# The two gate products of a recurrence, from two full-array fp32 matmuls to four quarter-array matmuls, with one result on swapped partition halves

## The chip, the cores and the metric

The kernel runs on one core of one Trainium2 chip. The metric is the device time of one execution, in microseconds. TensorE (PE) does the matmuls, PEld is its weight load, VectorE is DVE, ScalarE is ACT, GpSimd is POOL, and SyncE (SP) issues most of the DMAs. PSUM has eight banks here, written `ps[:, bank, :]`, each 128 partitions by 512 fp32 values.

## The reference

A trunk block over 512 tokens of width 1024: a mixer with three branches (banded attention, a spatial gate, a gated linear recurrence), then a mixture of 16 experts. The change touches only the two gates of the recurrence, whose matrices are block diagonal: 8 blocks of 64 by 64 over 512 channels.

```python
def block_diag_linear(x, w, bias):
    b, s, _ = x.shape
    y = jnp.einsum('bshi,hij->bshj', x.reshape(b, s, C_BLOCKS, C_BLOCK_DIM), w)
    return y.reshape(b, s, C_WIDTH) + bias

def rg_lru(x, w_a, b_a, w_x, b_x, lam):
    r = jax.nn.sigmoid(block_diag_linear(x, w_a, b_a)).astype(jnp.float32)
    i = jax.nn.sigmoid(block_diag_linear(x, w_x, b_x))
    log_a = -LRU_C * r * jax.nn.softplus(-lam.astype(jnp.float32))
    a = jnp.exp(log_a)
    mult = jnp.sqrt(jnp.maximum(-jnp.expm1(2.0 * log_a), 0.0))
    bterm = mult * (i * x).astype(jnp.float32)
    _, h = lax.associative_scan(_lin_rec_combine, (a, bterm), axis=1)
    return h.astype(x.dtype)
```

## The kernel before

Everything lies transposed in the stage that matters: channels on the partitions, the 512 tokens along the free dimension. The 512 channels of the recurrence are four groups of 128, and each group holds two of the 64-channel blocks. The stage runs over four pairs `j` (`NPAIR` = 4). One pair is two attention heads, 128 channels of the spatial gate and 128 channels of the recurrence. Each pair has five weight blocks, r = XR, KK, QQ, UU, XG. For a block TensorE does 24 matmuls of 512 columns (L1052 to L1054: the fp32 product is made of three, with a high and a low part of each operand). ACT makes the high part of a weight block three blocks ahead (`split_hi`, L371), and POOL the low part (`split_lo`, L383). After the four pairs comes the stage of the branch gates (`B_GATE`), whose first quarter holds the last steps of attention.

Between the blocks of pair `j` each engine does, in its own fixed order, a step of the attention of pair `j-1`: scores on TensorE (L1146, a head's 64 partitions of `kT` and `qT` for each product, the two heads in two PSUM banks), bias and maximum on DVE (L1582 to L1599), exponential on ACT (L738), normalising on DVE (L1608, L1610), transposes on TensorE (L1157) and the product with v (L1174, 128 partitions by 64 weight columns, the two heads in the two partition halves of one bank).

The gates come in the same order. Behind block QQ, TensorE multiplies `conv` (128 channels by 512 tokens, plain fp32) by `wa_diag` and by `wx_diag`, two 128 by 128 matrices in whose diagonal quarters the blocks lie and which are zero elsewhere (L1199 into bank 2, L1201 into bank 3). In step UU, ACT takes them: L810 makes `rgate`, L813 `igate`, then L818 `decay` and L822 `rgate` again. DVE goes on in `recurrence_in`: L1643 needs `igate`, L1646, L1647 and L1649 need L822, and behind them in DVE's order stand L1608 and L1610 of the attention. In step XG, ACT does a square root (L827) and a gelu (L829), each with a table load; in the next XR, DVE's L1661 makes the product of the branch, and the attention goes on. Every engine runs its list in program order; semaphores hold an instruction until what it needs is done.

In the profile one fp32 matmul of the program is two MATMUL records. The three-part matmuls are one record each. The buffer named `igate_decay` holds `igate` and `decay`.

## Time and profile before

| | us |
|---|---|
| median of 3 runs | 791.48 |
| lowest, highest | 791.05, 791.95 |
| the profiled execution | 791.86 |
| its span in the trace | 789.3 |
| TensorE busy | 764.9 (97% of the span) |
| DVE, ACT, POOL busy | 493.4, 450.4, 208.8 |

The page of the profile gives busy time and the chain of work that ended last. The timeline lists instructions with start, length and what ended an idle time before them; the list of waits sums these idle times. A TensorE record starts when its matmul enters the array, and its length includes the way through it, so a stream is measured from start to start and not by the lengths.

### The profile page before, as it was taken

Reading aid. Unit: us, or ns where it says so; the run is one execution under the profiler, and the core shown is the slowest. Engines: PE = TensorE matmul, PEld = TensorE weight load, DVE = VectorE, ACT = ScalarE, POOL = GpSimd, SP = SyncE. Lnnn points to the kernel's source line nnn. Section 1 sums busy time; section 2 is a strip of 40 time slices with the busy share of each in tenths; the row PEclk is TensorE's granted clock in tenths of the full one; section 3 lists DMA queues with packets and bytes.
Section 4 is the critical chain, followed back from the end, with each engine's and each line's share of the span. In section 5 each row is a group of like instructions: output and inputs, shape, how many; then the busy total and the mean of one; then the engine's idle time right before and its main releaser. Section 6 shows DMA issues by size and latency. Waiting matters only on the chain.

```text
span 789.3 us, 10839 instructions
## 1 busy us (share of the span) xinstructions
PE 764.9 (97%) x3739; PEld 622.0 (79%) x3739; DVE 493.4 (63%) x702; ACT 450.4 (57%) x590; POOL 208.8 (26%) x124
## 2 busy tenths in 40 slices
PE   7999999999999999999999999999999999999994
PEld 4788777777787888888888788887778888888782
DVE  5704476576644302322022668999999999999888
ACT  5244656565553323323221546887888887888862
POOL 3644433232233444344442522000000000000033
PEclk9999999999999999999999999999999999999998
DMA  8569999782122253323327537999999999999965
GB/s 299 183 215 386 365 333 388 276 329 81 54 81 81 81 193 100 108 81 105 102 86 264 194 114 275 404 409 408 409 410 409 409 410 409 409 409 356 395 253 205
DMA packets 134318, 206.74 MB, mean 262 GB/s; under 512 B 10813, under 2 KB 65669, under 8 KB 134278
## 3 DMA queue, kind: packets, MB, share of 16 engines
q1 hardware_dynamic: 126084, 188.80, 65.7%
q10 hardware_dynamic: 5890, 9.04, 3.1%
q0 software_dynamic: 2304, 8.39, 2.9%
q8 instruction: 24, 0.39, 0.2%
q14 instruction: 16, 0.13, 0.0%
HBM read 157.95 MB, written 48.25 MB: 261 GB/s over the span
## 4 chain that ended last, share of the span: by engine, by line
PE 82%; DVE 7%; ACT 2%; ACTq 2%; issue 2%; DMA 2%; POOL 2%; DVEq 0%; SPq 0%; POOLq 0%
PE ps L1052 24%; PE ps L1054 24%; PE ps L1053 24%; DVE w_lo L389 3%; PE ps L1342 2%; PE ps L1146 1%; PE ps L1174 1%; PE ps L1157 1%; PE ps L1295 1%; POOL raw_mg L656 1%; PE ps L1269 1%; DMA x<-in_x 1%; PE ps L1349 1%; ACTq L877 1%; DVE xT_lo L1959 1%
## 5 line engine op out<-in xcount | busy, mean ns | idle before, releaser
L383 POOL TENSOR_TENSOR w_lo<-raw,w_hi 128x1024 fp32r<-128x1024 f32 x72 | 173.6, 2414 | 253.1 <-ACT w_hi L371 253.1
L371 ACT ACTIVATE w_hi<-raw 128x1024 fp32r<-128x1024 f32 x73 | 76.9, 1058 | 191.9 <-PE ps L1054 164.4
L1052 PE MATMUL ps<-xn_hi,w_hi 128*128 128x512 f32 x352 | 140.6, 399 | 0.0
L1054 PE MATMUL ps<-xn_hi,w_lo 128*128 128x512 f32 x352 | 137.2, 390 | 0.0
L1053 PE MATMUL ps<-xn_lo,w_hi 128*128 128x512 f32 x352 | 137.1, 389 | 0.0
L1052 PE MATMUL ps<-w_hi,xT_hi 128*128 128x512 f32 (+1 forms) x248 | 97.0, 391 | 2.2 <-DVE w_lo L389 2.2
L1054 PE MATMUL ps<-w_hi,xT_lo 128*128 128x512 f32 (+1 forms) x248 | 95.2, 384 | 0.0
L1053 PE MATMUL ps<-w_lo,xT_hi 128*128 128x512 f32 (+1 forms) x248 | 94.9, 383 | 0.0
L656 POOL DMA_INDIRECT raw_mg<-slots,slot_idx x7 | 7.8, 1117 | 280.4 <-DMA slots<-y_tile 278.6
L1052 PEld LDWEIGHTS ps<-xn_hi,w_hi 128*128 128x128 f32 x352 | 66.1, 188 | 16.2 <-issue 2.0
L1053 PEld LDWEIGHTS ps<-xn_lo,w_hi 128*128 128x128 f32 x352 | 66.1, 188 | 14.0 <-issue 1.0
L1054 PEld LDWEIGHTS ps<-xn_hi,w_lo 128*128 128x128 f32 x352 | 66.1, 188 | 14.1
L1716 DVE SCALAR_TENSOR_TENSOR macc<-raw,ps 128x512 f32<-128x512 f32 x16 | 11.0, 688 | 94.0 <-PE ps L1054 93.8
L389 DVE TENSOR_TENSOR w_lo<-raw_mg,w_hi 128x1024 fp32r<-128x1024 f32 x57 | 67.7, 1221 | 1.0 <-ACT w_hi L378 0.7
L378 ACT ACTIVATE w_hi<-raw_mg 128x1024 fp32r<-128x1024 f32 x57 | 59.2, 1056 | 8.3 <-PE ps L1054 8.3
L1052 PEld LDWEIGHTS ps<-w_hi,xT_hi 128*128 128x128 f32 x248 | 46.6, 188 | 12.8 <-DVE w_lo L389 4.3
L389 DVE TENSOR_TENSOR w_lo<-raw,w_hi 128x1024 fp32r<-128x1024 f32 x43 | 51.3, 1220 | 5.9 <-ACT w_hi L378 5.8
L1054 PEld LDWEIGHTS ps<-w_hi,xT_lo 128*128 128x128 f32 x248 | 46.6, 188 | 9.2
L378 ACT ACTIVATE w_hi<-raw 128x1024 fp32r<-128x1024 f32 x43 | 44.9, 1057 | 14.8 <-PE ps L1054 10.9
L1053 PEld LDWEIGHTS ps<-w_lo,xT_hi 128*128 128x128 f32 x248 | 46.7, 188 | 8.4
L1052 PE MATMUL ps<-w_hi,hT_hi 128*128 128x512 f32 x128 | 51.2, 400 | 0.6 <-DVE hT_lo L1966 0.6
L1053 PE MATMUL ps<-w_lo,hT_hi 128*128 128x512 f32 x128 | 49.9, 390 | 0.0
(311 smaller groups left out, 1476.3 us busy)
## 6 DMA issues: line engine op xcount, KB each, us to landing
slots<-raw SPq DMA_DIRECT2D x65, 512.0 KB, 7.2
raw<-in_w_in SPq DMA_DIRECT2D x52, 512.0 KB, 4.1
raw_mg<-in_exp_w_down SPq DMA_DIRECT2D x35, 512.0 KB, 11.0
raw<-in_exp_w_gate SPq DMA_DIRECT2D x29, 512.0 KB, 11.6
raw_a<-in_exp_w_gate SPq DMA_DIRECT2D x26, 512.0 KB, 11.0
raw_c<-in_exp_w_up SPq DMA_DIRECT2D x24, 512.0 KB, 11.9
raw_mg<-in_exp_w_up SPq DMA_DIRECT2D x22, 512.0 KB, 11.1
raw<-in_exp_w_up SPq DMA_DIRECT2D x15, 512.0 KB, 11.7
```

The costliest lines, as they stand in the source:

```text
L371: nc.scalar.activation(w_hi[:, b % HI_SLOTS, :], raw_buf(b), ACT.Copy)\
L378: nc.scalar.activation(w_hi[:, (8 + r) % HI_SLOTS, :], buf, ACT.Copy).then_inc(S["hi_act"], 1)
L383: eng.tensor_tensor(w_lo[:, b % HI_SLOTS, :], raw_buf(b), w_hi[:, b % HI_SLOTS, :].bitcast(F32), ALU.subtract)\
L389: nc.vector.tensor_tensor(w_lo[:, (8 + r) % HI_SLOTS, :], place(at, r)[0], w_hi[:, (8 + r) % HI_SLOTS, :].bitcast(F32), ALU.subtract)\
L656: pool.indirect_dma_start(dst, None, slots, bass.IndirectOffsetOnAxis(ap=slot_idx[:, 2 * t + k:2 * t + k + 1], axis=0))\
L877: act.dma_start(router_w[:, :, NG:], a["router_exp_w"][0].rearrange("(k p) n -> p k n", p=P))\
L1052: pe.matmul(dst, hi_l, hi_r, start=start, stop=False)
L1053: pe.matmul(dst, hi_l, lo_r, start=False, stop=False)
L1054: return pe.matmul(dst, lo_l, hi_r, start=False, stop=stop)
L1146: mm = pe.matmul(score_home(g, h)[:, home + k0:home + k1], qT[rows, jp % 2, i * P:(i + 1) * P], kT[rows, jp % 2, k0:k1], start=True, stop= ...
L1342: mm = pe.transpose(ps[:, 3 + k // 4, (k % 4) * P:(k % 4 + 1) * P], rows[:, k * P:(k + 1) * P], ident[:, :])
L1716: dve.scalar_tensor_tensor(out=macc[:, 1, :], in0=gate_buf[:, g % 3, :], scalar=1.0, in1=ps[:, 2 + c, :], op0=ALU.add, op1=ALU.mult)\
```

## The change

The zero quarters of the two matrices are no longer multiplied. For each half `h` of the partitions there is one 64 by 64 matmul for each gate, again plain fp32 with 512 columns, so four instead of two. The results for `wa_diag` go to the half of bank 2 where they went before. The results for `wx_diag` go to the other half of bank 3, so each of the four has a quarter of the array for itself: (rows 0 to 63, columns 0 to 63), (0 to 63, 64 to 127), (64 to 127, 64 to 127) and (64 to 127, 0 to 63). ACT then takes `igate` with two instructions of 64 partitions, which put the halves back in place. The semaphore `gates_ps` rises by 2 behind the last matmul, instead of by 1 behind each; ACT waited for both before, too.

```diff
-                        act.activation(igate[:, :], ps[:, 3, :], ACT.Tanh, scale=0.5,
-                                       bias=par[:, PAR_BX + j:PAR_BX + j + 1])\
-                           .then_inc(S["gates_done"], 1)
+                        for h in range(2):
+                            own, other = (slice(n * 64, (n + 1) * 64) for n in (h, 1 - h))
+                            half = act.activation(igate[own, :], ps[other, 3, :], ACT.Tanh, scale=0.5,
+                                                  bias=par[own, PAR_BX + j:PAR_BX + j + 1])
+                        half.then_inc(S["gates_done"], 1)
...
-                        pe.matmul(ps[:, 2, :], wa_diag[:, j, :], conv[:, :], start=True, stop=True)\
-                          .then_inc(S["gates_ps"], 1)
-                        pe.matmul(ps[:, 3, :], wx_diag[:, j, :], conv[:, :], start=True, stop=True)\
-                          .then_inc(S["gates_ps"], 1)
+                        for h in range(2):
+                            own, other = (slice(n * 64, (n + 1) * 64) for n in (h, 1 - h))
+                            for bank, w_diag, to in ((2, wa_diag, own), (3, wx_diag, other)):
+                                mm = pe.matmul(ps[to, bank, :], w_diag[own, j, own], conv[own, :],
+                                               start=True, stop=True)
+                        mm.then_inc(S["gates_ps"], 2)
```

TensorE behind block QQ of the last pair (j = 3), before: the transposes and scores of the attention, the two gate matmuls, the first matmuls of block UU.

```order
L1157 MATMUL ps<-ident,probs 128x128 x3
L1146 MATMUL ps<-kT,qT 128x128 [waits biased]
L1146 MATMUL ps<-kT,qT 128x128 x3
L1199 MATMUL ps<-conv,wa_diag 128x512 [waits b_mid,diag_in,conv_done]
L1201 MATMUL ps<-conv,wx_diag 128x512
L1052 MATMUL ps<-xn_hi,w_hi 128x512 [waits taken,lo_pool]
```

The same place now.

```order
L1159 MATMUL ps<-ident,probs 128x128 x3
L1148 MATMUL ps<-kT,qT 128x128 [waits biased]
L1148 MATMUL ps<-kT,qT 128x128 x3
L1204 MATMUL ps<-conv,wa_diag 64x512 [waits b_mid,diag_in,conv_done]
L1204 MATMUL ps<-conv,wx_diag 64x512
L1204 MATMUL ps<-conv,wa_diag 64x512
L1204 MATMUL ps<-conv,wx_diag 64x512
L1054 MATMUL ps<-xn_hi,w_hi 128x512 [waits taken,lo_pool]
```

Two rows have become four in the same place, and nothing else on TensorE has moved.

ACT in step UU of the same pair, before: the exponentials of the attention, the gates, the next weight block.

```order
L738 ACTIVATE probs,att<-probs,att 128x256
L810 ACTIVATE rgate<-ps,par 128x512 [waits b_mid,chan_done,gates_ps]
L813 ACTIVATE igate_decay<-ps,par 128x512
L818 ACTIVATE igate_decay<-rgate,chan 128x512 [waits chan_done,gates_done]
L822 ACTIVATE rgate<-rgate,chan 128x512 [waits decay_done]
L371 ACTIVATE w_hi<-raw 128x1024 [waits w_used,raw_in2]
```

The same place now.

```order
L738 ACTIVATE probs,att<-probs,att 128x256
L810 ACTIVATE rgate<-ps,par 128x512 [waits b_mid,chan_done,gates_ps]
L815 ACTIVATE igate_decay<-ps,par 64x512 x2
L820 ACTIVATE igate_decay<-rgate,chan 128x512 [waits chan_done,gates_done]
L824 ACTIVATE rgate<-rgate,chan 128x512 [waits decay_done]
L371 ACTIVATE w_hi<-raw 128x1024 [waits w_used,raw_in2]
```

One more instruction stands ahead of `decay` and of everything behind it. DVE's and POOL's rows are the same as before.

## Rows read from the trace of the kernel before

**Rows 1.** The page, busy time: engine, us, share of span, instructions.

```profile
PE 764.9 (97%) x3739; PEld 622.0 (79%) x3739; DVE 493.4 (63%) x702; ACT 450.4 (57%) x590; POOL 208.8 (26%) x124
```

**Rows 2.** TensorE's waits: waiting instruction, releaser, total us, times, longest.

```profile
PE ps L1146 <- DVE att L1599: 1.7, 2, 1.0
PE ps L1157 <- DVE probs L1610: 1.0, 1, 1.0
```

**Rows 3.** TensorE's timeline, gates of j = 0: start, length, instruction, [idle before].

```profile
78.14 1.02 PE L1199 MATMUL ps<-conv,wa_diag 128*128 128x512 f32 x2
79.00 1.02 PE L1201 MATMUL ps<-conv,wx_diag 128*128 128x512 f32 x2
...
80.09 0.40 PE L1053 MATMUL ps<-xn_lo,w_hi 128*128 128x512 f32 x1
80.32 0.40 PE L1054 MATMUL ps<-xn_hi,w_lo 128*128 128x512 f32 x1
```

**Rows 4.** TensorE's timeline, scores and gates of j = 3.

```profile
187.97 0.71 PE L1146 MATMUL ps<-kT,qT 64*128 64x128 f32 x8
...
190.67 0.39 PE L1053 MATMUL ps<-xn_lo,w_hi 128*128 128x512 f32 x1
```

**Rows 5.** TensorE's timeline, the product with v ahead of these gates.

```profile
186.04 0.39 PE L1054 MATMUL ps<-xn_hi,w_lo 128*128 128x512 f32 x1
186.36 0.32 PE L1174 MATMUL ps<-probsT,v_rows 128*64 128x128 f32 x1
186.37 0.32 PE L1174 MATMUL ps<-macc,v_rows 128*64 128x128 f32 x1
186.52 0.27 PE L1174 MATMUL ps<-probsT,v_rows 128*64 128x128 f32 x1
...
187.18 0.27 PE L1174 MATMUL ps<-probsT,v_rows 128*64 128x128 f32 x1
```

**Rows 6.** TensorE's timeline, scores between two blocks of j = 1.

```profile
118.32 1.15 PE L1146 MATMUL ps<-kT,qT 64*128 64x256 f32 x12
119.40 0.50 PE L1052 MATMUL ps<-xn_hi,w_hi 128*128 128x512 f32 x1
119.74 0.39 PE L1053 MATMUL ps<-xn_lo,w_hi 128*128 128x512 f32 x1
```

**Rows 7.** ACT's timeline, steps UU and XG of j = 3.

```profile
192.65 0.67 ACT L810 ACTIVATE rgate<-ps,par 128x512 f32<-128x512 f32 x1
193.22 0.68 ACT L813 ACTIVATE igate_decay<-ps,par 128x512 f32<-128x512 f32 x1
...
194.64 0.81 ACT L822 ACTIVATE rgate<-rgate,chan 128x512 f32<-128x512 f32 x1
196.19 1.06 ACT L371 ACTIVATE w_hi<-raw 128x1024 fp32r<-128x1024 f32 x1 [0.73 <-PE ps L1054]
...
201.72 0.62 ACT L738 ACTIVATE probs<-probs,att 128x384 f32<-128x384 f32 x1 [3.51 <-DVE att L1599]
```

**Rows 8.** DVE's timeline, the same steps.

```profile
195.56 0.69 DVE L1646 TENSOR_TENSOR conv<-igate_decay 128x512 f32<-128x512 f32 x1 [0.94 <-ACT rgate L822]
...
197.01 0.43 DVE L1649 TENSOR_SCALAR rgate<-rgate 128x512 f32<-128x512 f32 x1
...
197.54 2.58 DVE L1610 TENSOR_SCALAR probs<-probs,att 128x256 f32<-128x256 f32 x2
200.04 0.34 DVE L1592 TENSOR_SCALAR probs<-ps,bias 128x128 f32<-128x128 f32 x1
```

**Rows 9.** POOL's timeline, the same steps.

```profile
197.32 2.39 POOL L383 TENSOR_TENSOR w_lo<-raw,w_hi 128x1024 fp32r<-128x1024 f32 x1 [7.31 <-ACT w_hi L371]
```

**Rows 10.** TensorE's timeline, attention behind pairs j = 2 and j = 3.

```profile
173.69 1.13 PE L1146 MATMUL ps<-kT,qT 64*128 64x256 f32 x8 [0.70 <-DVE att L1599]
...
212.79 0.66 PE L1157 MATMUL ps<-ident,probs 128*128 128x128 f32 x4 [0.95 <-DVE probs L1610]
...
214.45 1.13 PE L1146 MATMUL ps<-kT,qT 64*128 64x256 f32 x8 [1.00 <-DVE att L1599]
```

**Rows 11.** DVE's timeline, the step of j = 1 that answers to L1592 in rows 8.

```profile
119.52 0.35 DVE L1592 TENSOR_SCALAR probs<-ps,bias 128x128 f32<-128x128 f32 x1 [0.96 <-PE ps L1146]
```

## The prediction

> **What bounds the kernel now.** I read the page first. TensorE is busy for 97% of the span [rows 1], so what is taken off TensorE's stream should come off the end, wherever TensorE isn't waiting. So the second view is the list of TensorE's waits. In the stage of the four pairs it has three: L1146 waits twice and L1157 once for DVE's part of the attention [rows 2]. The timeline shows where they stand: 0.70 us at 173.69, behind pair j = 2, and 0.95 and 1.00 us at 212.79 and 214.45, behind pair j = 3 [rows 10]. At these two places DVE and ACT, and not TensorE, set the time. The gates of j = 2 and j = 3 lie ahead of them, and the change adds work to just that chain. So the question is not only what the four matmuls cost, but who gets the benefit in each pair.
>
> **TensorE, price of the old matmuls.** L1199 starts at 78.14 and L1201 at 79.00: 0.86 us for one fp32 matmul of 512 columns. From 78.14 to L1053 at 80.09 is 1.95 us, of which L1052 has 0.23 (the distance to the next row), so both gates take 1.72 us [rows 3]. This holds for j = 0, where full-array work stands ahead. In the others, scores stand ahead: from L1146 at 187.97 to L1053 at 190.67, less 0.23, is 2.47 us for scores, gates and the changes between them [rows 4].
>
> **TensorE, price of the new ones.** Each of the four streams the same 512 columns, so each alone costs 0.86 us. All depends on how many run side by side. No row shows four quarters, but two show halves. L1174 uses two column halves of the array: its records for the two heads start together (186.36 and 186.37), and the eight starts of each head come 0.11 us apart ((187.18 - 186.52) / 6) [rows 5], a quarter of 0.43 (half of 0.86) for a quarter of the columns, for both heads at once. L1146 uses two row halves: six matmuls, two of 256 columns and four of 128, are 1024 columns, 1.72 us in a row and 0.86 side by side; from 118.32 to the next work at 119.40 is 1.08 us [rows 6]. So both ways of halving give a factor of two in fp32. I take it that they combine, and put the four at 0.86 us; the other end is 3.44 us (four in a row).
>
> Changing how the array is divided costs something. Into column halves: L1054 at 186.04 plus 0.23 is 186.27, the first record comes at 186.36, and the second 0.16 behind it instead of 0.11 [rows 5], 0.14 in all. Out of row halves: 1.08 - 0.86 = 0.22, and then 119.74 - 119.40 = 0.34 instead of 0.23 [rows 6], 0.33 in all. For j = 0 the new sum is 0.14 + 0.86 + 0.33 = 1.33, a gain of 0.39 us. For j = 1 to 3 it is 0.43 for the scores (512 columns, halved), a change from one division to another of between 0.14 and 0.33, then 0.86 + 0.33, or 1.76 to 1.95: a gain of 0.52 to 0.71, say 0.6 us. If leaving quarters cost nothing, the gain would be 0.72 and up to 1.04.
>
> On this the Trainium skill says two things, in TensorE: Matmul & The Clock Gate, section "Measured speedup vs the span model": sixteen small tiles in a 4 by 4 grid ran 10.6 times as fast, which would put four quarters at one pass. What it says against is a rival, below.
>
> **ACT, one instruction more.** L813 stands 0.57 us behind L810 (193.22 - 192.65) [rows 7]. It becomes two of 64 partitions and the same 512 columns. No ACT row has fewer than 128 partitions; half price (nothing added) is the lower bound, full price (0.57 us added) the upper. I take the upper one: the nearest row is L738, which with 384 columns takes 0.62 against L810's 0.67 with 512 [rows 7], so even fewer columns save little. In j = 0 this is not felt: no wait of TensorE follows. In j = 1, L1592 of DVE waits 0.96 us for TensorE's scores [rows 11], more than 0.57, so what is late there is still TensorE. Hence j = 0 and j = 1 keep their gains: 0.39 + 0.6 = 1.0 us.
>
> **The chain behind j = 3, and in the same way j = 2.** L810 starts at 192.65, over a microsecond after the old gates are through (the block's L1053 is on at 190.67 [rows 4]), so it doesn't start earlier when TensorE is faster. L822 moves from 194.64 to 195.21 and ends at 196.02. L371 waited for block UU, 0.73 us [rows 7]; with TensorE some 0.6 earlier that is over by 195.6, and it starts at 196.0 instead of 196.19, when ACT is free. POOL's L383 starts 1.13 us behind it, and ran from 197.32 to 199.71 [rows 9]: now 197.13 to 199.52. DVE's L1649 moves from 197.01 to 197.58, and now falls inside that. What this means can be read from L1610: two of them took 2.58 us from 197.54, and L1592 behind them began at 200.04, 0.33 after POOL's end [rows 8]. DVE stood still while POOL ran. Before, only the two L1610 were caught; now L1649 is caught ahead of them. When POOL ends, L1649 has to finish (0.33), and L1608 and the two L1610 follow; from L1649 to L1610 is 0.53 [rows 8], and the pair needs about 0.2 free. So L1592 starts at 199.52 + 0.33 + 0.53 and up to 0.2 more, 200.4 to 200.6, against 200.04: 0.35 to 0.55 later, say 0.45. So POOL's lock hides little of ACT's 0.57. From there on the chain has no slack: L738 at 201.72 waits for DVE [rows 7], and it ends in the waits of rows 10. The price is 0 if L1649 gets through ahead of POOL and the chain gains what L371 gained, and about 1.05 if L1647, which is due only 0.3 us ahead of POOL, is caught as well.
>
> TensorE, arriving 0.6 us earlier at 212.79 and 173.69, waits 0.6 longer and is then released 0.45 later than before. So in j = 2 and j = 3 the gain of the matmuls is not seen at all, and ACT's loss is.
>
> **The sum.** -0.39 - 0.6 + 0.45 + 0.45 = -0.1 us. The later stages start from TensorE's place and slide with it. The profiled execution of 791.86 becomes 791.76; it lay 0.38 above the median, so the prediction is 791.48 - 0.1 = 791.4 us. The measurement tells 0.2% (1.6 us) from no change.
>
> **Rivals.** *Two at a time instead of four.* In every row above where two run side by side they share the same rows of the array (L1174), or write two banks (L1146). Here the two matmuls for `wa_diag` are of different row halves and write one bank, and so do the two for `wx_diag`. If that keeps them apart, the four take 1.72 us. Then j = 0 loses 0.14 + 1.72 + 0.33 - 1.72 = 0.47, j = 1 loses 0.43 + 0.14 + 1.72 + 0.33 - 2.47 = 0.15, POOL ends at 199.9 and not 199.52, so the chain loses 0.85 each time: +2.3 us, 793.8. It decides against the change from the point where the four need more than about 1.2 us. For it speaks that the kernel always gives the two row halves two banks; against it that L1174's two heads write one bank together, in different partitions, as here [rows 5]. 18%. This is what the Trainium skill states in TensorEngine Tiling (Array Packing), section "Gotcha 1: PSUM Pressure": different row tiles can't access the same bank simultaneously. No trace here has this case.
>
> *The swap does nothing: all four in a row.* 3.44 us: j = 0 loses 2.2, j = 1 1.9, and in j = 2 and j = 3 TensorE becomes late itself, by 1.9 less the 0.7 that it idled, or by what the chain then adds, about 1.2 each: +6.5 us, 798.0. Rows 5 and 6 speak against it. 6%.
>
> *The chain doesn't lose.* The halves cost half, or POOL's lock hides the 0.57, and the changes of division cost less: j = 0 and j = 1 give up to 0.72 + 0.71, the chain up to 0.1 each: -1.0 to -1.6 us, about 790.2. 12%.
>
> **How the numbers follow.** The forecast (four side by side, gains kept in two pairs and lost in two, 791.4, from 790.8 with the chain at its cheapest to 792.6 with L1647 caught) has 61%. With 18, 6 and 12% for the rivals, 3% are left for something slower that I don't name. Faster by over 0.2% needs the far end of the last rival, and something that I don't see: 10%. Slower by over 0.2%: most of the first rival (13%), the second and the unnamed: 22%. Within: 68%. The range of 790.0 to 794.0 holds all but four in a row and some of the unnamed; its own range for the likeliest is 790.8 to 792.6.
>
> **What would show it.** Four records of the new line within some 10 ns of each other, twice, 0.43 us apart; the stretch from the first of them to L1053's successor at j = 0 near 1.2 us instead of 1.95 - 0.23. ACT's two halves 0.57 us apart each. At j = 3, DVE's counterpart of L1649 as long as L1610 is now. The two waits for L1599 and the one for L1610 longer by 1 us each place, with TensorE's busy time lower by about 2 us. I am wrong if the four come in two steps, if the waits behind j = 2 and j = 3 don't grow, or if a wait of TensorE appears behind j = 1.

## The result: 0.85% slower, with a faster TensorE

The changed kernel takes 796.85 us in the median of six runs (795.95 to 805.3), the kernel before 791.38 in the same comparison (791.02 to 793.77). The ratio is 1.0085, with a 95% interval from 1.0045 to 1.0125. A repeat with more runs (e1, below) gives 1.0048, 1.0029 to 1.0068. The forecast was 791.4 us, the range 790.0 to 794.0: the time lies above the range. The profiled execution of the changed kernel took 805.3 us (span 803.5, mean granted clock 0.983), the one of before 791.86 (789.3, 0.996).

The page of the changed kernel has two lines that tell most of it. The first answers to [rows 1]; the second is the clock granted to TensorE in 40 slices of the span, in tenths:

```profile
PE 770.9 (96%) x3755; PEld 625.1 (78%) x3755; DVE 497.7 (62%) x702; ACT 452.9 (56%) x594; POOL 209.7 (26%) x124
PEclk9999998998989999999999999999999999999998
```

ACT has four instructions more and 2.5 us more work. TensorE has less to stream and is nevertheless busy for 6 us longer. The second line shows why: where the kernel before has a 9 in every slice but the last, there are now three more 8s, all in the stage with the four pairs.

TensorE's waits in the stretch of the pairs (waiting instruction, releaser, total us, times, longest), to be held against [rows 2]:

```profile
PE ps L1159 <- DVE probs L1614: 4.8, 2, 2.7
PE ps L1148 <- DVE att L1603: 2.5, 3, 1.0
PE ps L1159 <- DVE probs_third L1614: 1.4, 1, 1.4
PE ps L1176 <- ACT probsT L748: 0.7, 1, 0.7
```

Three waits of 2.7 us in all have become seven, of 9.4 us. The window from 57 to 257 us of the changed kernel says the same by engine (sum; busy us and count of PE, PEld, DVE, ACT, POOL; granted clock; DMA share; GB/s):

```profile
57.00:257.00 200.00, 190.46 (x1009) 149.25 (x1008) 114.84 (x198) 112.48 (x195) 66.55 (x31) 0.95 0.64 233
```

In the same window of the kernel before, TensorE was busy for 197.35 us at a granted clock of 1.00. So 7 us go to idle time, and 0.95 over 200 us is a further 10 us of full clock lost.

**The new gates themselves are better than forecast.** TensorE's timeline of the changed kernel at j = 0, where [rows 3] shows before (start, length, instruction):

```profile
77.54 0.39 PE L1056 MATMUL ps<-xn_hi,w_lo 128*128 128x512 f32 x1
77.86 0.64 PE L1204 MATMUL ps<-conv,wa_diag 64*64 64x512 f32 x1
77.87 0.64 PE L1204 MATMUL ps<-conv,wx_diag 64*64 64x512 f32 x1
77.87 0.64 PE L1204 MATMUL ps<-conv,wa_diag 64*64 64x512 f32 x1
77.88 0.64 PE L1204 MATMUL ps<-conv,wx_diag 64*64 64x512 f32 x1
78.34 0.59 PE L1204 MATMUL ps<-conv,wa_diag 64*64 64x512 f32 x1
...
78.88 0.50 PE L1054 MATMUL ps<-xn_hi,w_hi 128*128 128x512 f32 x1
79.22 0.39 PE L1055 MATMUL ps<-xn_lo,w_hi 128*128 128x512 f32 x1
```

Four records start within 0.02 us of each other, and four more 0.48 later: all four quarters run side by side. From the end of the matmul ahead (77.54 + 0.23) to L1054's own place (79.22 - 0.23) is 1.22 us, where it was 1.72: a gain of 0.50 us at j = 0. In the other three pairs scores stand ahead. From L1148 at 196.57 (j = 3) to L1054's own place (198.57 - 0.23) is 1.77 us, where it was 2.47 [rows 4]: a gain of 0.70 us, and about the same at j = 1 and j = 2. Together that is 2.6 us.

**What the chain behind j = 3 looks like now.** ACT, DVE and POOL of the changed kernel, where [rows 7], [rows 8] and [rows 9] show before:

```profile
201.26 0.67 ACT L810 ACTIVATE rgate<-ps,par 128x512 f32<-128x512 f32 x1
201.96 1.38 ACT L815 ACTIVATE igate_decay<-ps,par 64x512 f32<-64x512 f32 x2
203.37 0.82 ACT L820 ACTIVATE igate_decay<-rgate,chan 128x512 f32<-128x512 f32 x1
```

```profile
206.59 2.51 DVE L1653 TENSOR_SCALAR rgate<-rgate 128x512 f32<-128x512 f32 x1
209.21 0.62 DVE L1614 TENSOR_SCALAR probs<-probs,att 128x256 f32<-128x256 f32 x2
209.74 0.34 DVE L1596 TENSOR_SCALAR probs<-ps,bias 128x128 f32<-128x128 f32 x1
```

```profile
206.06 2.76 POOL L383 TENSOR_TENSOR w_lo<-raw,w_hi 128x1024 fp32r<-128x1024 f32 x1 [7.43 <-ACT w_hi L371]
```

The clamp L1653 (the maximum of `rgate` with 0, L1649 before) took 0.43 us before and takes 2.51: it stands still until POOL's L383 ends at 208.82. This is what the text below calls the lock, and an instruction of DVE that is held by it is caught. From L810 to L1596 it is 8.48 us, where L810 to L1592 was 7.39 (200.04 - 192.65, [rows 7, 8]).

**And what TensorE makes of it.** Its timeline behind pairs j = 1, 2 and 3, with the idle time before each instruction, where [rows 10] has three waits:

```profile
132.33 0.66 PE L1176 MATMUL ps<-probsT,v_rows 128*64 128x128 f32 x8 [0.71 <-ACT probsT L748]
...
135.06 1.12 PE L1159 MATMUL ps<-ident,probs 128*128 128x128 f32 x4 [2.08 <-DVE probs L1614]
...
136.72 2.08 PE L1148 MATMUL ps<-kT,qT 64*128 64x256 f32 x8 [0.54 <-DVE att L1603]
...
177.68 0.66 PE L1159 MATMUL ps<-ident,probs_third 128*128 128x128 f32 x4 [1.42 <-DVE probs_third L1614]
...
179.34 2.08 PE L1148 MATMUL ps<-kT,qT 64*128 64x256 f32 x8 [1.00 <-DVE att L1603]
...
222.47 0.66 PE L1159 MATMUL ps<-ident,probs 128*128 128x128 f32 x4 [2.75 <-DVE probs L1614]
...
224.13 2.08 PE L1148 MATMUL ps<-kT,qT 64*128 64x256 f32 x8 [1.00 <-DVE att L1603]
```

Behind j = 2 it idles 2.4 us instead of 0.7, behind j = 3 3.75 instead of 1.95, and behind j = 1 3.3 instead of none. After each of the three, L1148's eight matmuls take 2.08 us, which take 1.13 in [rows 10]. That is the clock: the windows of the changed kernel behind j = 1 (columns as above) show it fall from full (2.4 GHz) to half (1.2 GHz) after the idle time, while TensorE has work again, and come back later. Finer windows put the whole stretch at half clock from about 134.5 to 141.3, 6.8 us, and it is as long behind j = 2 and j = 3.

```profile
132.00:134.00 2.00, 0.66 (x8) 0.42 (x8) 2.00 (x1) 1.56 (x2) 1.73 (x1) 1.00 1.03 420
134.00:136.00 2.00, 0.94 (x4) 0.72 (x4) 1.93 (x8) 0.00 (x0) 0.00 (x0) 0.62 1.01 401
136.00:138.00 2.00, 1.46 (x7) 1.19 (x8) 1.94 (x5) 1.39 (x5) 0.00 (x0) 0.50 1.12 346
...
142.00:144.00 2.00, 2.00 (x11) 1.64 (x10) 1.89 (x4) 0.00 (x0) 0.00 (x0) 1.00 0.83 243
```

So my theory after the result was: the gates gain, ACT's second half pushes DVE's clamp into POOL's L383, DVE's part of the attention comes late behind three pairs, TensorE idles, and for that its clock falls, which costs again. The rivals were that the quarters themselves cost (through the swap, or their changes of division), or that ACT's split alone explains all. One more question was whether the 805.3 of the profiled execution stands for the kernel at all.

### The profile page after: what moved, and what is told of

The parts are those of the page before. It is cut to its first block, busy times and chain, and to the rows that moved or that the text cites. A ratio compares the mean times of both kernels' runs of the same rounds, so it can differ in the third digit from the quotient of the medians.

```text
span 803.5 us, 10875 instructions
## 1 busy us (share of the span) xinstructions
PE 770.9 (96%) x3755; PEld 625.1 (78%) x3755; DVE 497.7 (62%) x702; ACT 452.9 (56%) x594; POOL 209.7 (26%) x124
## 4 chain that ended last, share of the span: by engine, by line
PE 66%; DVE 10%; ACT 6%; SPq 5%; DMA 4%; issue 3%; POOL 2%; ACTq 2%; DVEq 0%; POOLq 0%
PE ps L1054 20%; PE ps L1056 20%; PE ps L1055 19%; SPq L469 4%; DVE w_lo L389 3%; DMA raw<-in_w_in 2%; PE ps L1346 2%; POOL w_lo L383 1%; ACT w_hi L371 1%; PE ps L1148 1%; PE ps L1299 1%; DVE rgate L1653 1%; POOL raw_mg L656 1%; PE ps L1273 1%; DMA raw_mg<-slots,slot_idx 1%
## 5 line engine op out<-in xcount | busy, mean ns | idle before, releaser
L383 POOL TENSOR_TENSOR w_lo<-raw,w_hi 128x1024 fp32r<-128x1024 f32 x72 | 174.5, 2427 | 264.9 <-ACT w_hi L371 264.9
L371 ACT ACTIVATE w_hi<-raw 128x1024 fp32r<-128x1024 f32 x73 | 76.7, 1056 | 196.7 <-PE ps L1056 165.4
L1054 PE MATMUL ps<-xn_hi,w_hi 128*128 128x512 f32 x352 | 141.6, 402 | 0.0
L1055 PE MATMUL ps<-xn_lo,w_hi 128*128 128x512 f32 x352 | 139.0, 395 | 0.0
L1056 PE MATMUL ps<-xn_hi,w_lo 128*128 128x512 f32 x352 | 138.9, 395 | 0.0
L1054 PE MATMUL ps<-w_hi,xT_hi 128*128 128x512 f32 (+1 forms) x248 | 97.2, 392 | 2.2 <-DVE w_lo L389 2.2
L1054 PEld LDWEIGHTS ps<-xn_hi,w_hi 128*128 128x128 f32 x352 | 67.5, 192 | 19.9 <-issue 5.8
L1054 PEld LDWEIGHTS ps<-w_hi,xT_hi 128*128 128x128 f32 x248 | 46.6, 188 | 12.8 <-DVE w_lo L389 4.3
L1054 PE MATMUL ps<-w_hi,hT_hi 128*128 128x512 f32 x128 | 51.4, 401 | 0.6 <-DVE hT_lo L1970 0.6
L1056 PE MATMUL ps<-w_hi,hT_lo 128*128 128x512 f32 x128 | 50.0, 391 | 0.0
```

Of the source, the lines that this page charges most:

```text
L371: nc.scalar.activation(w_hi[:, b % HI_SLOTS, :], raw_buf(b), ACT.Copy)\
L383: eng.tensor_tensor(w_lo[:, b % HI_SLOTS, :], raw_buf(b), w_hi[:, b % HI_SLOTS, :].bitcast(F32), ALU.subtract)\
L1054: pe.matmul(dst, hi_l, hi_r, start=start, stop=False)
L1055: pe.matmul(dst, hi_l, lo_r, start=False, stop=False)
L1056: return pe.matmul(dst, lo_l, hi_r, start=False, stop=stop)
```

## The experiments

In the table below, "idle" is TensorE's idle time from 57 to 287 us of the profiled execution, and "clock" is the full-clock time that the granted clock took there: the length of each stretch times (1 - granted). Both columns are of one execution. In after, e1, e4, e6, e7 and e10 the profiled execution took the longest of all the kernel's runs, so these columns stand for that run and not for the median.

| kernel | idle | clock | median us (range, runs) | before, same chip | ratio, 95% |
|---|---|---|---|---|---|
| before | 2.65 | 0 | 791.38 (791.02 to 793.77, 6) | | |
| after | 9.54 | 10.25 | 796.85 (795.95 to 805.3, 6) | 791.38 | 1.0085, 1.0045 to 1.0125 |
| e1 after again | 8.07 | 5.15 | 796.1 (795.61 to 800.14, 7) | 792.12 | 1.0048, 1.0029 to 1.0068 |
| e2 ACT's split alone | 4.50 | 1.7 | 794.66 (794.17 to 795.48, 10) | 792.12 | 1.0029, 1.0016 to 1.0042 |
| e3 quarters, one ACT instruction | 4.26 | 1.7 | 793.24 (790.26 to 795.15, 10) | 792.12 | 1.0012, 0.9996 to 1.0027 |
| e4 clamp out of POOL's reach | 6.58 | 5.1 | 795.6 (794.12 to 798.54, 7) | 792.12 | 1.0039, 1.0015 to 1.0064 |
| e7 after, TensorE kept busy | 3.40 | 3.4 | 796.66 (793.95 to 799.17, 5) | 791.83 | 1.0059, 1.0039 to 1.0079 |
| e8 quarters without the swap | 2.64 | 0 | 792.78 (791.55 to 794.28, 10) | 791.83 | 1.0012, 1.0001 to 1.0023 |
| e6 before, igate late | 2.10 | 1.7 | 792.69 (790.06 to 794.02, 10) | 791.83 | 0.9998, 0.9981 to 1.0014 |
| e10 e6 with ACT's split | 0.0 | 0 | 788.96 (787.66 to 791.07, 12) | 792.2 | 0.9954, 0.9938 to 0.9969 |
| e5 after, igate late | 0.28 | 0 | 786.75 (786.05 to 788.54, 4) | 791.83 | 0.9947, 0.9928 to 0.9966 |
| e9 e5 again | 0.28 | 0 | 786.8 (786.26 to 787.03, 6) | 792.2 | 0.9929, 0.9904 to 0.9954 |
| e11 e5, one ACT instruction | 3.07 | 0 | 790.46 (789.56 to 792.16, 10) | 792.2 | 0.9979, 0.9963 to 0.9994 |

The verdicts go by the ratio, which compares with the runs of before that stand beside a kernel's own; the medians of two different rows differ by the chip's own drift as well.

### e1: the changed kernel once more

No edit. 

> The changed kernel once more, for a second profile beside the kernel before on the same chip. In the first profile TensorE waits 2.1 to 2.7 us longer than before behind each of j = 1, 2 and 3, and its granted clock falls to 0.50 for about 5 us behind each of them. Theory A (the chain through ACT and DVE is later, TensorE idles, then its clock falls): every run has the longer waits, and the number of clock falls varies between runs, 795 to 805 us. Theory B (the quarter matmuls themselves cost the time): the time would lie in and right behind them. 796 to 798.

Measured: 796.1 us, and a profile with less lost clock than the first (5.15 us instead of 10.25), idle 8.07. The runs of the changed kernel go together with their clock. Of the seven runs on record with the first result, that of 795.95 us lost 4.8 us of full clock over its span, that of 797.46 us 7.2, that of 800.2 us 9.6, and that of 805.3 us 13.7. Span less lost clock is 787.7 to 789.8 for all of them. In e1's own comparison it is 787.2 to 789.6 (median 787.6) for the changed kernel and 784.4 to 788.1 (median 786.3) for before. So there are two parts: one that does not hang on the clock, 1.3 us by the medians in e1's comparison and 2.5 for the first seven runs (median 788.8) against the same runs of before, and a clock loss that differs from run to run, 4.8 to 8.8 us in e1's runs. Runs of before lose 3.2 us at the least (in its profile nearly all of it at the very end, behind 783.6), but 13 of these 24 lose more, up to 7.1. The 805.3 is not the kernel's usual time, only its worst. What the page of that one execution shows of the clock is therefore more than the median carries.

### e2 and e3: each half of the change alone

e2 is the kernel before with ACT's second gate in two instructions, no halves swapped:

```diff
-                        act.activation(igate[:, :], ps[:, 3, :], ACT.Tanh, scale=0.5,
-                                       bias=par[:, PAR_BX + j:PAR_BX + j + 1])\
-                           .then_inc(S["gates_done"], 1)
+                        for h in range(2):
+                            own, other = (slice(n * 64, (n + 1) * 64) for n in (h, 1 - h))
+                            half = act.activation(igate[own, :], ps[own, 3, :], ACT.Tanh, scale=0.5,
+                                                  bias=par[own, PAR_BX + j:PAR_BX + j + 1])
+                        half.then_inc(S["gates_done"], 1)
```

> The kernel before with only ACT's part of the change: igate is taken in two instructions of 64 partitions, halves not swapped, the two matmuls are the old full ones. Theory A: ACT is 0.97 us later at decay as in the changed kernel, DVE's clamp of rgate is caught behind POOL, the waits behind j = 2 and j = 3 grow by 1 to 2 us, and the time rises by 2 to 6 us, to 793 to 797. Theory B: 791.4, no change, since TensorE's work is the old one.

e3 is the changed kernel with one ACT instruction over all 128 partitions, so that the halves are not put back:

```diff
-                        for h in range(2):
-                            own, other = (slice(n * 64, (n + 1) * 64) for n in (h, 1 - h))
-                            half = act.activation(igate[own, :], ps[other, 3, :], ACT.Tanh, scale=0.5,
-                                                  bias=par[own, PAR_BX + j:PAR_BX + j + 1])
-                        half.then_inc(S["gates_done"], 1)
+                        act.activation(igate[:, :], ps[:, 3, :], ACT.Tanh, scale=0.5,
+                                       bias=par[:, PAR_BX + j:PAR_BX + j + 1])\
+                           .then_inc(S["gates_done"], 1)
```

> The changed kernel with igate taken by one ACT instruction of 128 partitions as before. The two halves of igate are then not put back in their places, so that part of the computation is left out. It is TensorE's part of the change alone. Theory A: the chain is as before, j = 0 and j = 1 gain 0.5 each and j = 2, 3 nothing, about 790.4; TensorE idles 0.6 us longer in two places, so a fall of the clock there may cost 2 to 3 us. Theory B: 796 to 798.

Measured: by the ratios e2 is 2.3 us slower than before, and e3 1.0 us (its interval just takes in no change). Both times fit theory A, e3's with one fall of the clock on top of its 790.4; but the chain of e3 is not as before, as shown below. With the faster matmuls alone, TensorE idles 1.6 us longer than before, so much of what the matmuls gain in the stage is waited away, and its clock fell once (1.7 us). What e3 lies above before is clock: span less lost clock has a median of 785.8 us, where before has 786.3. The split alone catches the clamp at j = 3 in the same way as the full change; DVE, then POOL, of e2:

```profile
198.87 2.50 DVE L1651 TENSOR_SCALAR rgate<-rgate 128x512 f32<-128x512 f32 x1
```

```profile
198.34 2.75 POOL L383 TENSOR_TENSOR w_lo<-raw,w_hi 128x1024 fp32r<-128x1024 f32 x1 [7.30 <-ACT w_hi L371]
```

The faster matmuls alone catch it too, behind j = 2 and j = 3, with ACT as it was. DVE, then POOL, of e3:

```profile
195.85 2.51 DVE L1651 TENSOR_SCALAR rgate<-rgate 128x512 f32<-128x512 f32 x1
```

```profile
195.44 2.64 POOL L383 TENSOR_TENSOR w_lo<-raw,w_hi 128x1024 fp32r<-128x1024 f32 x1 [6.58 <-ACT w_hi L371]
```

L810 stands at 191.49 there, so POOL starts 3.95 us behind it, where it was 4.67 (197.32 - 192.65): the 0.73 us that L371 waited for TensorE [rows 7] are gone. With the clamp caught instead of the normalising pair, the scores on DVE come 0.92 us behind POOL's end (199.00 - 198.08), where it was 0.33. But POOL also ends earlier, 6.59 us behind L810 instead of 7.06. So from L810 to the scores it is 7.51 us, only 0.12 more than before. In e2 POOL ends 7.41 us behind L810, in the changed kernel 7.56, and there the chain has 8.33 and 8.48: the later ACT makes the difference.

In the times the two halves add up to the whole of e1 within the intervals (1.0029 and 1.0012 against 1.0048). In the traces they don't: they add 1.9 and 1.6 us of idle time, the whole 5.4 (e1) or 6.9. The difference stands at j = 1. There the clamp of e2 still gets through ahead of POOL (DVE, then POOL, of e2):

```profile
118.34 0.43 DVE L1651 TENSOR_SCALAR rgate<-rgate 128x512 f32<-128x512 f32 x1
```

```profile
119.25 2.50 POOL L383 TENSOR_TENSOR w_lo<-raw,w_hi 128x1024 fp32r<-128x1024 f32 x1 [5.58 <-ACT w_hi L371]
```

In the changed kernel it does not (ACT, DVE, POOL):

```profile
109.05 1.06 ACT L371 ACTIVATE w_hi<-raw 128x1024 fp32r<-128x1024 f32 x1 [8.86 <-DMA raw<-in_w_in]
...
118.89 1.05 ACT L371 ACTIVATE w_hi<-raw 128x1024 fp32r<-128x1024 f32 x1
```

```profile
120.54 2.50 DVE L1653 TENSOR_SCALAR rgate<-rgate 128x512 f32<-128x512 f32 x1
```

```profile
120.02 2.74 POOL L383 TENSOR_TENSOR w_lo<-raw,w_hi 128x1024 fp32r<-128x1024 f32 x1 [4.26 <-ACT w_hi L371]
```

The kernel before has the clamp at 117.40 and POOL at 119.19, 1.79 us apart; e2 still 0.91; in the changed kernel POOL is 0.52 ahead. An ACT L371 earlier in the pair waits for its weights' DMA until 109.05 (106.56 in before), ACT then works without a break, and its last L371, which releases POOL, follows straight on the gate work. Of the kernels so far only those with both halves of the change have this collision. In e1 that DMA landed at 107.94, and still the clamp (119.40) came 0.52 behind POOL (118.88), so its exact time doesn't decide. But the landing may have a part in it: in e3 it came at 106.28, with L810 at 112.46 and POOL at 117.90. From such an L810 the clamp of the changed kernel would be due at 117.78 (5.32 behind it, 120.54 - 115.22), 0.12 ahead of POOL by this estimate. No run separates the two, and why the DMA lands later than in before I did not settle.

### e4: the clamp out of POOL's reach

DVE's instructions that read PSUM were never seen to stand still under POOL. So the sum ahead of the clamp goes to PSUM, and the clamp reads it there:

```diff
-                link(dve.scalar_tensor_tensor(out=rgate[:, :], in0=conv[:, :], scalar=1.0, in1=rgate[:, :],
+                link(dve.scalar_tensor_tensor(out=ps[:, 2, :], in0=conv[:, :], scalar=1.0, in1=rgate[:, :],
...
-                dve.tensor_scalar(rgate[:, :], rgate[:, :], 0.0, None, ALU.max).then_inc(S["mult_in"], 1)
+                dve.tensor_scalar(rgate[:, :], ps[:, 2, :], 0.0, None, ALU.max).then_inc(S["mult_in"], 1)
```

and TensorE waits for `mult_in` before it writes that bank again. 

> The changed kernel, with DVE's sum for rgate written into PSUM bank 2 and the clamp (the maximum with 0) read from there. DVE instructions that read PSUM ran on while POOL ran, in the trace of before; the clamp from SBUF took 2.5 us instead of 0.43. Theory A with the lock as the multiplier: the clamp takes 0.5 to 0.7 us even while POOL runs, the chain is 1 us late or less instead of 3, TensorE idles less, no or one clock fall, 791 to 794. If the lock isn't what matters: 796 to 798.

Measured: 795.6 us, outside the ranges of both theories (791 to 794, 796 to 798) and, by the ratios 1.0039 and 1.0048, not told apart from e1. So the time alone neither supports the lock nor speaks against it; the profile does. TensorE idles 6.58 us instead of 8.07, and the clock took as much as in e1. DVE, then POOL, at j = 3:

```profile
200.11 0.69 DVE L1654 TENSOR_SCALAR rgate<-ps 128x512 f32<-128x512 f32 x1
200.91 1.83 DVE L1615 TENSOR_SCALAR probs<-probs,att 128x256 f32<-128x256 f32 x2
```

```profile
199.57 2.75 POOL L383 TENSOR_TENSOR w_lo<-raw,w_hi 128x1024 fp32r<-128x1024 f32 x1 [7.43 <-ACT w_hi L371]
```

The clamp is free of POOL, at 0.69 us inside POOL's instruction. But the next pair on DVE, L1615, which reads SBUF, is held until POOL ends at 202.32. The lock does not belong to one instruction; it is a fixed end that the next such instruction has to wait for. To avoid it, all of DVE's work up to L1615 must be through before POOL starts.

### e5 and e6: take the second gate off the chain

The decay needs only the first gate; the second enters behind the clamp. So ACT computes it last, and DVE's sum with it moves to the start of the recurrence. e5 is this on the changed kernel, e6 on the kernel before:

```diff
-                dve.wait_ge(S["gates_done"], 2 * j + 2)
-                link(dve.scalar_tensor_tensor(out=igate[:, :], in0=igate[:, :], scalar=1.0, in1=conv[:, :],
-                                              op0=ALU.add, op1=ALU.mult))
...
-                link(dve.tensor_tensor(conv[:, :], decay[:, :], decay[:, :], ALU.mult))
-                link(dve.scalar_tensor_tensor(out=rgate[:, :], in0=conv[:, :], scalar=1.0, in1=rgate[:, :],
+                link(dve.tensor_tensor(ps[:, 2, :], decay[:, :], decay[:, :], ALU.mult))
+                link(dve.scalar_tensor_tensor(out=rgate[:, :], in0=ps[:, 2, :], scalar=1.0, in1=rgate[:, :],
...
+                dve.wait_ge(S["gates_done"], 2 * j + 2)
+                link(dve.scalar_tensor_tensor(out=igate[:, :], in0=igate[:, :], scalar=1.0, in1=conv[:, :],
+                                              op0=ALU.add, op1=ALU.mult))
```

The last three lines stand at the start of `recurrence(j)`, the others in `recurrence_in`. On ACT the unchanged lines of igate stand behind those of the second `rgate`. TensorE waits for `mult_in` in step XG before it writes bank 2 again.

> The changed kernel with igate taken behind decay and rgate on ACT instead of ahead of them, and with DVE's product of igate and conv moved to where igate is used next (in step XG); the square of decay goes to PSUM bank 2, since conv is needed longer. Same work, other order. Theory A (ACT's later decay and the lock behind it set the time): the clamp is now due 1.5 to 2 us earlier than in the changed kernel and is through ahead of POOL, TensorE's waits behind the pairs nearly vanish and with them the falls of the clock, 786 to 789. If the order on ACT doesn't matter: 796.

> The same new order on ACT and DVE, but with the kernel before's two full matmuls and one igate instruction. Theory A: the 2.65 us of waits of before vanish, about 789; e5 is then below it by four times the gain of the quarters, 0.5 us each, or 2 us. If e6 is at or below e5, the quarters bring nothing even with the chain out of the way.

Measured: e5 and its repeat e9 are the fastest kernels of the study, 786.75 and 786.8 us; idle time falls from 9.54 to 0.28, and the clock loss is gone. From L810 to the first score operation is now 4.92 us instead of 8.48. e6 did not do as expected (789): 792.69, no change against before (ratio 0.9998). Its chain is 7.11 us, not 4.9, and DVE and POOL at j = 3 say why:

```profile
197.00 2.79 DVE L1611 TENSOR_SCALAR probs<-probs,att 128x256 f32<-128x256 f32 x2
```

```profile
197.25 2.39 POOL L383 TENSOR_TENSOR w_lo<-raw,w_hi 128x1024 fp32r<-128x1024 f32 x1 [7.29 <-ACT w_hi L371]
```

The pair L1611 starts 0.25 us ahead of POOL. The first of the two gets through, the second is held, and the pair takes 2.79 us. In e5, POOL starts later, since ACT has one more instruction ahead of its L371. That suggested a test with an odd forecast: more work on ACT should make e6 faster.

### e9, e10, e11: which part carries it

e9 is e5 once more. e10 is e6 with ACT's igate in two instructions of 64 partitions, halves not swapped, and the full matmuls kept:

```diff
-                        act.activation(igate[:, :], ps[:, 3, :], ACT.Tanh, scale=0.5,
-                                       bias=par[:, PAR_BX + j:PAR_BX + j + 1])\
-                           .then_inc(S["gates_done"], 1)
+                        for h in range(2):
+                            own, other = (slice(n * 64, (n + 1) * 64) for n in (h, 1 - h))
+                            half = act.activation(igate[own, :], ps[own, 3, :], ACT.Tanh, scale=0.5,
+                                                  bias=par[own, PAR_BX + j:PAR_BX + j + 1])
+                        half.then_inc(S["gates_done"], 1)
```

e11 is e5 with the edit of e3: one ACT instruction, halves not put back.

> The kernel of e5 once more, with more rounds: igate behind decay and rgate, quarters on TensorE. In e5, DVE's two normalising instructions of pair 3 were through 0.1 us behind POOL's start, because ACT's two late igate instructions held POOL's input back. If that is what makes it fast, it repeats: 786 to 787.5, with no wait of TensorE over 0.5 us behind the pairs and hardly any loss to the clock.

> The order of e5 and e6 with the two full matmuls, and igate in two instructions of 64 partitions (halves not swapped). It has more work than e6 (792.7), by one ACT instruction for each pair. Theory A with POOL's lock as the hinge: the extra instruction stands behind what DVE waits for and ahead of the weight block that POOL waits for, so DVE gets through ahead of POOL as in e5; the waits vanish, and the time is that of e5 plus four times 0.5 us, 788 to 789.5. If only the amount of work on ACT counts: 793 or more.

> The kernel of e5 with one igate instruction of 128 partitions; the halves of igate are not put back, so that part of the computation is left out. It has less work than e5, by one ACT instruction for each pair. Theory A with the lock as the hinge: POOL starts 0.8 us earlier and catches DVE's normalising instructions of pair 3 as in e6, the waits come back, 789 to 792, slower than e5 with less to do. If only the amount of work counts: 786 or less.

Measured: e9 786.8, e10 788.96, e11 790.46 us, all three as expected. One ACT instruction more makes e6 about 3.5 us faster (0.9998 and 0.9954 by the ratios), and one less makes e9, which is e5's kernel, 3.7 us slower beside the same runs of before. The same two rows, DVE's normalising pair and then POOL, of e9, e10 and e11, in this order:

```profile
194.10 0.62 DVE L1615 TENSOR_SCALAR probs<-probs,att 128x256 f32<-128x256 f32 x2
...
194.64 2.42 POOL L383 TENSOR_TENSOR w_lo<-raw,w_hi 128x1024 fp32r<-128x1024 f32 x1 [7.57 <-ACT w_hi L371]
```

```profile
198.32 0.62 DVE L1613 TENSOR_SCALAR probs<-probs,att 128x256 f32<-128x256 f32 x2
...
198.72 2.48 POOL L383 TENSOR_TENSOR w_lo<-raw,w_hi 128x1024 fp32r<-128x1024 f32 x1 [7.44 <-ACT w_hi L371]
```

```profile
195.91 2.56 DVE L1613 TENSOR_SCALAR probs<-probs,att 128x256 f32<-128x256 f32 x2
...
195.48 2.58 POOL L383 TENSOR_TENSOR w_lo<-raw,w_hi 128x1024 fp32r<-128x1024 f32 x1 [6.60 <-ACT w_hi L371]
```

With 0.54 and 0.40 us between the two the pair takes 0.62; with POOL 0.43 ahead it takes 2.56. And e10 less e9 is 2.2 us: this is what the quarters are worth once nothing else is late; the gates' own gains in the trace are 0.50 + 3 x 0.70 = 2.6 us.

### e7: TensorE kept busy through the waits

The changed kernel with six matmuls into a free bank ahead of each of the three waits:

```diff
+                if g in (3, 8, 13):
+                    for n in range(6):
+                        pe.matmul(ps[:, 3, :], xn_hi[:, 0, 0:P], xn_hi[:, 0, :], start=True, stop=True)
```

> The changed kernel with six matmuls of no use (0.23 us each, into PSUM bank 3, which is free there) in TensorE's order just ahead of the wait for the normalised scores behind pairs 1, 2 and 3. They add 1.4 us of work in a place where TensorE idles 1.4 to 2.8 us. Theory A, with the fall of the clock as a cost of its own behind the idle time: the granted clock no longer falls behind most pairs, and the time drops by 2 to 4 us, to 792.5 to 794. If the idle time alone is the cost: 796 to 797, unchanged.

Measured: 796.66 us (793.95 to 799.17), no better than the changed kernel. In its profile the falls behind j = 1 and j = 2 are gone, but one stayed (and one of 3.4 us came at 445.6, far behind the stage). TensorE, behind j = 3:

```profile
215.52 0.66 PE L1162 MATMUL ps<-ident,probs 128*128 128x128 f32 x4 [1.14 <-DVE probs L1617]
...
217.18 2.08 PE L1148 MATMUL ps<-kT,qT 64*128 64x256 f32 x8 [1.00 <-DVE att L1606]
```

Here 1.14 + 1.00 us of idle time were followed by half clock, while 0.95 + 1.00 in [rows 10] and 1.16 + 1.00 at the same place in e11 were not. The added work fills idle time but ends too late or too early for part of it, so the test was not clean: it does not price the clock by itself. For that the spread of the changed kernel's own runs stands, where the same program differs mostly by the clock (span less lost clock still varies by 2.1 to 2.4 us).

### e8: the quarters without the swap

The four quarter matmuls in another order, the second gate on its own halves. The two matmuls of one gate, of different row halves, now follow each other and write one bank:

```diff
+                        for bank, w_diag in ((2, wa_diag), (3, wx_diag)):
+                            for own in (slice(0, 64), slice(64, 128)):
+                                mm = pe.matmul(ps[own, bank, :], w_diag[own, j, own], conv[own, :],
+                                               start=True, stop=True)
+                        mm.then_inc(S["gates_ps"], 2)
```

ACT's igate stays one instruction. 

> The change without the swap: four matmuls of 64 by 64 as in the changed kernel, but the results of wx_diag on their own halves and igate taken by one instruction of 128 partitions. Two of the four use the same quarter, so at most two run side by side: 1.72 us plus 0.3 to 0.5 for changing the division, no gain. Theory A: the chain on ACT is the old one, 791.5 to 792.5. Theory B (small matmuls cost in themselves): 795 or more.

Measured: 792.78 us, 1.0 us above before and 0.3 above the range of theory A. TensorE at j = 0:

```profile
78.60 0.39 PE L1054 MATMUL ps<-xn_hi,w_lo 128*128 128x512 f32 x1
78.92 1.08 PE L1201 MATMUL ps<-conv,wa_diag 64*64 64x512 f32 x4
79.83 1.02 PE L1201 MATMUL ps<-conv,wx_diag 64*64 64x512 f32 x4
80.78 0.50 PE L1052 MATMUL ps<-xn_hi,w_hi 128*128 128x512 f32 x1
```

Two quarters of 512 columns take 0.91 us (79.83 - 78.92), not 1.72: two row halves do run side by side into one bank, when they write different partitions. But only two run at once here, so the gates take 1.72 plus the changes of division, 2.05 in all, and lose 0.33 at j = 0; in the other pairs, where the division changes anyhow, they lose 0.15. That is 0.8 us in all, near the 1.0 measured. The swap is what allows four, and it is paid on ACT.

## Why the prediction was wrong, by its own steps

- **TensorE, price of the new ones: right.** Four side by side, 1.22 us against the forecast 1.33 at j = 0, so a gain of 0.50 and not 0.39. In pair j = 3 scores and gates take 1.77 us against the forecast 1.76 to 1.95, a gain of 0.70 in the forecast's 0.52 to 0.71. The rivals "two at a time" and "all four in a row" fell with the records at 77.86, and e8 says why the first could: a common bank does not separate two row halves. The Trainium skill states the opposite in TensorEngine Tiling (Array Packing), section "Gotcha 1: PSUM Pressure"; the runs differ from it, with 0.91 us for two of 0.86.
- **ACT, one instruction more: too small.** Forecast 0.57 us, measured 0.97: from L810 to the decay is 2.11 us (203.37 - 201.26), where it was 1.14. Each half costs as much as a full instruction (0.69), and from the first half to the decay are 1.41 us (203.37 - 201.96), 0.70 for each, where a full one has 0.57. The first half stands 0.70 behind L810 (201.96 - 201.26). In e2, without the swap, it stands 0.57 behind it as a full one does, and the split adds 0.82 instead of 0.97; so about 0.15 comes with the swapped halves. The upper bound of that term, "full price", was not a bound.
- **The chain behind j = 3 and j = 2: the mechanism right, the size 2.4 times too small.** The clamp is caught by POOL, as said, but the chain grew by 1.09 us, not 0.45. Two terms make the difference. POOL started 4.80 us behind L810 (206.06 - 201.26), where I had 4.48 (197.13 - 192.65): 0.32 later, the most of ACT's missing 0.40. And L383 ran for 2.76 us instead of 2.39; I took the 2.39 of [rows 9] as fixed. It starts while DVE's L1651, the sum ahead of the clamp, still has 0.50 us to go. With 0.38 left (e3) it ran for 2.64, with 0.22 left of a normalising instruction (e10) for 2.48: the more was left, the longer POOL's own instruction. What follows POOL's end was right: 0.92 us (209.74 - 208.82), where I had 0.33 + 0.53 and up to 0.2. The waits grew by 1.7 and 1.8 us, where I had 1.05 each.
- **"j = 0 and j = 1 keep their gains": the step that failed.** I reckoned with 0.96 us of slack at one instruction of DVE [rows 11], and did not ask where the clamp of j = 1 stands against POOL. It stood 1.79 us ahead; now it is caught. From L810 to L1596 it is 8.47 us at j = 1 where it was 6.47 to L1592 (119.52 - 113.05), so the chain grew by 2.0 us and not by 0.57, twice the slack, and L810 itself starts later, 115.22 against 113.05 (114.08 in e1). TensorE idles 3.3 us (2.35 in e1) where it idled none. A wait of TensorE behind j = 1 was what the forecast itself named as its refutation.
- **Missing from the sum altogether: the clock.** The sum gives TensorE's idle time its own length as price. In the profiles, after many of the places with 1.6 to 3.8 us of idle time in two or three pieces, the granted clock is 0.50 for 3.4 or for 6.8 us, at a price of 1.7 or 3.4 us. For the run of 805.3 us this is the largest term, 10.25 us in the stretch. For the usual run it is less: over the whole span the median run of e1 lost 6.4 us and the median run of before beside it 3.9, so 2.5 us of e1's 4.0 are clock.

The account closes roughly, with 2.6 us for the gates. The last product with v of the stage starts at 257.3 us in before, 269.7 in the changed kernel and 264.5 in e1. For e1, idle +5.4, clock +5.15 and gates -2.6 give +8.0, measured +7.2. For the changed kernel's own profile, idle +6.9, clock +10.25 and gates -2.6 give +14.5, measured +12.4; idle time inside a stretch of half clock is counted in both terms, which I estimate at 1.3 us there and 0.5 in e1, and 0.8 stays unexplained. For e9, idle -2.4 and gates -2.6 give -5.0, measured -5.4. Behind that point the rest of the kernel took 533.8 us in the changed kernel and in e1, against 532.0 in before: 1.7 us more that the experiments did not look into.

What stays open is what exactly makes the clock fall. The lengths of the waits do not decide it: 0.68 + 1.00 us in e6 and 1.14 + 1.00 in e7 were followed by half clock, 0.95 + 1.00 in the profile of before and 1.16 + 1.00 in e11 were not. Behind j = 2 the changed kernel waited 1.42 + 1.00 and fell, and e1, the same program, waited 1.42 + 1.00 and did not (L1148's eight matmuls took 1.14 us). The unprofiled runs of before must have fallen now and then as well, since about half of them lost more clock than its profile.

## What to carry to other kernels

Before counting what a faster engine saves, look at who waits behind it: here the faster matmuls gave 2.2 us once the chain of ACT and DVE was short (e9 against e10; with the shorter chain 0.7% faster than before), and the change cost 0.5 to 0.85% when the chain was lengthened. Where two engines lock each other out, write down for every repetition of the loop, and not only for the one already late, which of them comes first and by how much; whether all of DVE's list gets through ahead of POOL decides by 2 us (7.11 us from L810 to the scores in e6, 4.98 in e10), and even more work on one engine can make the kernel faster (e10 against e6). And price idle time of TensorE by more than its length, as a range, since the same program fell in some executions and not in others.

## What the runs showed of the hardware

- Four fp32 matmuls of 64 by 64 with 512 columns run side by side in four quarters of the array, with the two records of each 0.48 us apart. In each of the two banks, each row half writes one half of the partitions. Between full-array matmuls the four take 1.22 us in all, of which 0.86 is the stream of 512 columns and about 0.36 going into and out of that division.
- An ACT instruction of 64 partitions takes 0.69 us, as long as one of 128 (0.67), and two of them take 1.41 us up to the start of the next instruction (1.39 in e2), where full ones stand 0.57 apart.
- DVE's clamp and normalising pair, from SBUF to SBUF, stand still until POOL's L383 ends (the clamp's 0.43 us became 2.51); a clamp that reads PSUM takes its 0.69 us inside it (e4). Not every instruction on SBUF is held: in before, TENSOR_REDUCE L1599 of 512 columns takes 0.69 us, RECIPROCAL L1608 0.16 and the small TENSOR_SCALAR L1561 0.15, inside L383 as outside. If POOL starts while the sum L1651 on SBUF has 0.50 us to go, POOL's takes 2.75 instead of 2.39 us; with 0.37 us to go of L1592, which reads PSUM, it took 2.41.
- The granted clock fell from 2.4 to 1.2 GHz after TensorE had been idle in several short pieces, none longer than 2.75 us, and stayed there for 3.4 or 6.8 us. The same waits did not always bring it, and the same program's runs differ mostly by that from 795.95 to 805.3 us.
